# Gate one-hots split between VectorE and ScalarE, gate products as rounded part and rest, and PSUM sums copied out in the prompt attention

## What is computed

```python
# prompt attention, per head: softmax over causal keys, then the values
p = jax.nn.softmax(sc, axis=-1)            # sc = q.k/sqrt(dh) + bias
o = jnp.einsum("bhqk,bkhd->bqhd", p, v32)
# PEER, per token: 8 heads pick 16 experts each, out of 128 x 128
eidx = jnp.take_along_axis(cidx, pos, axis=-1)     # i1 * 128 + i2
g = jax.nn.softmax(top, axis=-1)
hid = jnp.einsum("thkd,td->thk", u_tab[eidx], xt)
a = g * jax.nn.gelu(hid, approximate=False)
out = jnp.einsum("thk,thkd->td", a, v_tab[eidx])
```

## Time and profile before

| | us |
|---|---|
| median of 3 runs (1883.18 to 1885.74) | 1885.15 |
| the profiled execution | 1886.61 |
| its span, first to last instruction | 1885.0 |

### The profile page before, as it was taken

The page is one execution under the profiler, slowest core; times in us unless marked ns, Lnnn a source line. Parts: engine busy times, 40 slices in busy tenths (PEclk is TensorE's granted clock), DMA queues, the critical chain, the costliest instruction groups (busy, mean ns, idle before and its releaser), DMA issues. The chain is left out here.

```text
span 1885.0 us, 30152 instructions
## 1 busy us (share of the span) xinstructions
PE 1701.0 (90%) x9914; PEld 1491.1 (79%) x9914; DVE 1438.2 (76%) x3371; ACT 683.1 (36%) x907; POOL 572.1 (30%) x508
## 2 busy tenths in 40 slices
PE   5997897779799999769989999998699999999995
PEld 3997643339699999769979999997588888888883
DVE  3334266524479989979989999997898999999985
ACT  3222032221434442344535455453333333333334
POOL 0010270000254543523333333333333333333330
PEclk8998898799799999979989999999799999999997
DMA  3242361152333332369997999999999999999992
GB/s 110 96 177 88 126 204 45 46 204 104 105 123 125 122 126 92 127 240 334 350 362 263 388 341 353 354 333 355 366 385 382 384 384 385 385 383 389 384 384 85
DMA packets 195214, 470.81 MB, mean 250 GB/s; under 512 B 17922, under 2 KB 100482, under 8 KB 192558
## 3 DMA queue, kind: packets, MB, share of 16 engines
q1 hardware_dynamic: 124014, 240.30, 36.1%
q0 software_dynamic: 50944, 178.96, 25.7%
q10 hardware_dynamic: 20160, 50.34, 6.9%
HBM read 411.97 MB, written 61.32 MB: 251 GB/s over the span
## 5 line engine op out<-in xcount | busy, mean ns | idle before, releaser
L226 PE MATMUL hp<-mid_hi,uhi 128*128 128x384 f32 x1024 | 355.8, 347 | 13.8 <-DVE ulo L1751 6.9
L227 PE MATMUL hp<-mid_lo,uhi 128*128 128x384 f32 x1024 | 346.6, 338 | 0.0
L228 PE MATMUL hp<-mid_hi,ulo 128*128 128x384 f32 x1024 | 345.1, 337 | 0.0
L226 PE MATMUL va<-vhi,ahi 128*128 128x512 f32 x768 | 299.7, 390 | 22.0 <-DVE alo L1957 22.0
L228 PE MATMUL va<-vhi,alo 128*128 128x512 f32 x768 | 299.5, 390 | 0.0
L227 PE MATMUL va<-vlo,ahi 128*128 128x512 f32 x768 | 299.5, 390 | 0.0
L1973 POOL DMA_INDIRECT gathered<-in_v_experts,idx_row x160 | 186.3, 1165 | 325.0 <-DVEq L1928 290.2
L1686 POOL DMA_INDIRECT gathered<-in_u_rows,idx_row x160 | 171.2, 1070 | 321.2 <-DVE hrow L1738 226.2
L226 PEld LDWEIGHTS hp<-mid_hi,uhi 128*128 128x128 f32 x1024 | 194.7, 190 | 18.0 <-DVE ulo L1751 9.1
L228 PEld LDWEIGHTS hp<-mid_hi,ulo 128*128 128x128 f32 x1024 | 194.3, 190 | 0.0
L227 PEld LDWEIGHTS hp<-mid_lo,uhi 128*128 128x128 f32 x1024 | 194.3, 190 | 0.0
(11 more groups left out here) (323 smaller groups left out, 3251.7 us busy)
## 6 DMA issues: line engine op xcount, KB each, us to landing
uw<-in_u_experts SPq DMA_DIRECT2D x128, 512.0 KB, 6.9
vw<-in_v_experts SPq DMA_DIRECT2D x128, 512.0 KB, 10.6
hidden_values<-gelu_out ACTq DMA_DIRECT2D x128, 192.0 KB, 5.9
gate_matrix<-gst ACTq DMA_DIRECT2D x12, 2048.0 KB, 13.2
mid_hi<-hidden_values SPq DMA_DIRECT2D x32, 768.0 KB, 11.9
mid_lo<-gate_matrix SPq DMA_DIRECT2D x32, 768.0 KB, 16.7
pw<-in_w_qk SPq DMA_DIRECT2D x16, 512.0 KB, 3.5
qw<-in_w_query SPq DMA_DIRECT2D x16, 512.0 KB, 4.7
```

Source lines behind the costliest of these rows:

```text
L226: nc.tensor.matmul(out, a_hi, b_hi, start=first, stop=False)
L227: nc.tensor.matmul(out, a_hi, b_lo, start=False, stop=False)
L228: return nc.tensor.matmul(out, a_lo, b_hi, start=False, stop=last)
```

## The change

In the gate stage:

- the transposed gates are kept as two parts: rounded to fp32r (by ScalarE) and the rest (by POOL). The transposed indices and gates lie over the used part of `I1`, `I2` and `GG`; `chunkT` has four columns a pick, copied by POOL in four pieces, with a new wait for ScalarE's progress (`first`)
- DVE builds `og` twice for each token, with the rounded gate and with the rest, and no `oh` any more; both in fp32r
- ScalarE builds `oh`: for each of four tokens |i - index| by an Abs with the index as bias (128 columns), then one Relu(1 - x) over the group's 512 columns, in fp32r. It does so two groups ahead, behind the copy of `gst`
- PE makes two fp32r products for each token, summed in PSUM, in place of one in fp32, and waits for `oh` and `first`.

In the prompt attention:

- ScalarE copies `DN` and `OT` out of PSUM (`move(j - 1)`, ahead of pair j's exponentials), and PE's `values(j, 0)` waits for that (`moved`) in place of `normed`
- DVE takes the reciprocal in two halves (`invert`), after blocks 0 and 1, and multiplies after block 1, both from SBUF; `split_hi` and `split_lo` come one block later
- the diagonals of pairs 4 to 7 are made by ScalarE, block by block
- `on` has two buffers; the copy of `OT` and the squares lie in a used part of `qkT`.

```diff
-            on = sb(st, "on", [P, SEQ])
-            sqt = sb(st, "sqt", [P, SEQ])
+            on = sb(st, "on", [P, 2, SEQ])
+            sqt, o_raw = qkT[:, 0, :SEQ], qkT[:, 1, :SEQ]
...
                     if i == 0 and j:
-                        pe.wait_ge(normed, j)
+                        pe.wait_ge(moved, j)
...
+                def invert(j, part):
+                    cols = slice(part * SEQ // 2, (part + 1) * SEQ // 2)
+                    dve.wait_ge(moved, j + 1)
+                    nc.vector.reciprocal(on[:, j % 2, cols], on[:, j % 2, cols]).then_inc(inv, 1)
+
                 def keep(j):
-                    dve.wait_ge(pv_mm, QB * (j + 1))
-                    if j:
-                        dve.wait_ge(o_lo, j)
-                    nc.vector.reciprocal(on[:], DN[:]).then_inc(inv, 1)
-                    dve.wait_ge(inv, j + 1)
-                    nc.vector.tensor_tensor(on[:], OT[:], on[:], ALU.mult).then_inc(normed, 1)
+                    dve.wait_ge(inv, 2 * (j + 1))
+                    nc.vector.tensor_tensor(on[:, j % 2], o_raw, on[:, j % 2], ALU.mult).then_inc(normed, 1)
...
-                        if i == 0 and j:
+                        if i < 2 and j:
+                            invert(j - 1, i)
+                        if i == 1 and j:
                             keep(j - 1)
-                        if i == 2 and j:
+                        if i == 3 and j:
                             split_lo(j - 1)
...
+                def diagonal(j, i):
+                    for u in range(2):
+                        act.wait_ge(max_done, unit(j, i, u) + 1)
+                        act.wait_ge(t_mm, unit(j - 2, QB - 1, u) + 1)
+                        last = nc.scalar.activation(diag[:, j % 2, u, i], ident[:], ACT.Copy, scale=negm[:, j % 2, u, i:i + 1])
+                        if i == QB - 1:
+                            last.then_inc(diag_done, 1)
...
+                def move(j):
+                    act.wait_ge(pv_mm, QB * (j + 1))
+                    if j:
+                        act.wait_ge(normed, j)
+                    if j >= 2:
+                        act.wait_ge(o_lo, j - 1)
+                    nc.scalar.activation(on[:, j % 2], DN[:], ACT.Copy)
+                    nc.scalar.activation(o_raw, OT[:], ACT.Copy).then_inc(moved, 1)
...
-            oh = sb(st, "oh", [P, RING, 4, P])
-            og = sb(st, "og", [P, RING, 4, P])
+            oh = sb(st, "oh", [P, RING, 4, P], F32R)
+            og = sb(st, "og", [P, RING, 4, 2, P], F32R)
...
                         pe.wait_ge(s["oh"], j * N2 + i + 1)
+                        pe.wait_ge(s["first"], j * N2 + i + 1 + GR)
                         pe.wait_ge(s["ev"], j * N2 + i + 1)
                         for k in range(4):
-                            last = nc.tensor.matmul(gp[i % 2][:, k], oh[:, i % RING, k], og[:, i % RING, k], start=True, stop=True)
+                            for q in range(2):
+                                last = nc.tensor.matmul(gp[i % 2][:, k], oh[:, i % RING, k], og[:, i % RING, k, q],
+                                                        start=q == 0, stop=q == 1)
...
-                    nc.gpsimd.tensor_copy(chunkT[:, u], slotT[:, :, bass.ds((2 * j + u) * CH, CH)]).then_inc(s["cut"], 1)
+                    if not first:
+                        pool.wait_ge(s["first"], (2 * j + u) * GR)
+                    for q in range(4):
+                        last = nc.gpsimd.tensor_copy(chunkT[:, u, q], GATES[q][:, bass.ds((2 * j + u) * CH, CH)])
+                    last.then_inc(s["cut"], 1)
...
-                        nc.vector.tensor_scalar(oh[:, i % RING, k], iota[:], col(1), None, ALU.is_equal)
-                        last = nc.vector.tensor_scalar(og[:, i % RING, k], iota[:], col(0), col(2), ALU.is_equal, ALU.mult)
+                        for q in range(2):
+                            last = nc.vector.tensor_scalar(og[:, i % RING, k, q], iota[:], col(0), col(2 + q), ALU.is_equal, ALU.mult)
...
+                def first_one_hot(j, i):
+
+                    u, r = groups[i]
+                    act.wait_ge(s["cut"], 2 * j + u + 1)
+                    act.wait_ge(s["mm"], j * N2 + i + 1)
+                    for k in range(4):
+                        last = nc.scalar.activation(oh[:, i % RING, k], iota[:], ACT.Abs, scale=-1.0,
+                                                    bias=chunkT[:, u, 1, 4 * r + k:4 * r + k + 1])
+                    last.then_inc(s["dist"], 1)
+                    act.wait_ge(s["dist"], j * N2 + i + 1)
+                    nc.scalar.activation(oh[:, i % RING], oh[:, i % RING].bitcast(F32), ACT.Relu, scale=-1.0, bias=1.0).then_inc(s["first"], 1)
...
                         nc.scalar.activation(gst[:, u, :, 4 * r:4 * r + 4].rearrange("p i t -> p t i"), gp[i % 2][:],
                                              ACT.Copy).then_inc(s["ev"], 1)
+                        if i + 2 < N2:
+                            first_one_hot(j, i + 2)
+                        elif not last:
+                            first_one_hot(j + 1, i + 2 - N2)
```

More of the change, by code:

```diff
@@ L675, in build @@
             stg = [sem(f"a_stg{u}") for u in range(4)]
-            s_mm, max_done, diag_done, t_mm, biased, e_done, pv_mm, inv, normed, o_hi, o_lo, summed, const_ld, const_ev = (
-                sem("a_" + n) for n in ("s_mm", "max", "diag", "t_mm", "biased", "e", "pv", "inv", "normed", "o_hi", "o_lo", "summed",
+            s_mm, max_done, diag_done, t_mm, biased, e_done, pv_mm, inv, moved, normed, o_hi, o_lo, summed, const_ld, const_ev = (
+                sem("a_" + n) for n in ("s_mm", "max", "diag", "t_mm", "biased", "e", "pv", "inv", "moved", "normed", "o_hi", "o_lo", "summed",
                                         "const_ld", "const_ev"))
@@ L865, in split_lo @@
                             dve.wait_ge(summed, j // 4 * 3 + j % 4 - 1)
[L866 removed]
+                        nc.vector.tensor_tensor(sqsum[:, j // 4], sqsum[:, j // 4], sqt, ALU.add).then_inc(summed, 1)
                 for i in range(QB):
@@ L895, in split_hi @@
                         act.wait_ge(summed, j // 4 * 3 + j % 4 - 1)
-                    nc.scalar.activation(sqt[:] if j % 4 else sqsum[:, j // 4], on[:], ACT.Square)
-                    nc.scalar.activation(mid_hi[:, j, :SEQ], on[:], ACT.Copy, scale=gO[:, j:j + 1]).then_inc(o_hi, 1)
+                    nc.scalar.activation(sqt if j % 4 else sqsum[:, j // 4], on[:, j % 2], ACT.Square)
+                    nc.scalar.activation(mid_hi[:, j, :SEQ], on[:, j % 2], ACT.Copy, scale=gO[:, j:j + 1]).then_inc(o_hi, 1)
+                def move(j):
[6 more added lines that the diff above has]
+                    nc.scalar.activation(o_raw, OT[:], ACT.Copy).then_inc(moved, 1)
                 for j in range(PAIRS):
+                    if j:
+                        move(j - 1)
                     for i in range(QB):
@@ L912, in _ @@
                                 nc.scalar.activation(ET[:, u, at[i]:at[i + 1]], ST[u][:, :n], ACT.Exp, scale=1.0 / SCALE8).then_inc(e_done, 1)
-                        if i == 1 and j:
+                        if j + 1 >= FOX and j + 1 < PAIRS:
+                            diagonal(j + 1, i)
+                        if i == 2 and j:
                             split_hi(j - 1)
+                move(PAIRS - 1)
                 split_hi(PAIRS - 1)
@@ L1612, in build @@
             tp = gp[0][:].rearrange("p a n -> p (a n)")[:, :TD]
-            names = ("tr", "trev", "cut", "oh", "mm", "ev", "part", "x2p", "tab", "idx", "dot", "hrow", "act")
+            names = ("tr", "trev", "cut", "oh", "dist", "first", "ghi", "glo", "mm", "ev", "part", "x2p", "tab", "idx", "dot", "hrow", "act")
             s = {n: sem("g_" + n) for n in names}
@@ L1787, in _ @@
                     act.wait_ge(s["tr"], i + 1)
-                    nc.scalar.activation(slotT[:, i], tp, ACT.Copy).then_inc(s["trev"], 1)
+                    if i == 2:
+                        nc.scalar.activation(rounded, tp.rearrange("p (a n) -> p a n", a=3), ACT.Copy).then_inc(s["ghi"], 1)
+                    nc.scalar.activation(slotT[i], tp, ACT.Copy).then_inc(s["trev"], 1)
                 act.wait_ge(x2r_spread, 16 * SG)
@@ L1793, in _ @@
                 act.sem_inc(stored[1], 16)
+                act.sem_inc(s["first"], GR)
+                def first_one_hot(j, i):
[8 more added lines that the diff above has]
+                    nc.scalar.activation(oh[:, i % RING], oh[:, i % RING].bitcast(F32), ACT.Relu, scale=-1.0, bias=1.0).then_inc(s["first"], 1)
+                first_one_hot(0, 0)
+                first_one_hot(0, 1)
                 def turn(j, half, last):
```

23 lines of the change are left out of this document (18 added, 5 removed).

## The result

| | before | after |
|---|---|---|
| median us | 1883.18 (1878.19 to 1885.74, 5 runs) | 1900.62 (1898.56 to 1906.16, 5 runs) |
| the profiled execution | 1886.61 | 1906.16 |
| its span | 1885.0 | 1904.5 |

The ratio is 1.0101, with a 95% interval of 1.0085 to 1.0117: 19.0 us slower (16 to 22). The spans differ by 19.5. The forecast was +19.9. Both profiled executions are the longest of their kernel's five runs, 3.4 us over the median before and 5.5 after.

What follows compares the result with a forecast made beforehand. It took DVE and PE to share the gate stage's bound, with DVE's lateness showing on PE. One-hots +23.4, waits -1, start +2 and attention -4.5 summed to +19.9 on 1885.15, giving 1905 us, range 1890 to 1926.

Steps and rivals of the forecast that it cites:

- Gate products on PE: Gate stage: 768 fp32r products replace 384 fp32 ones at the same 0.11 us load pace, 0; bounds -43 and +1.
- One-hots on VectorE: Gate stage: eight `og` replace four `oh` and four `og` a group, +0.244 us each over 96 groups, +23.4 us.
- First one-hots on ScalarE: Gate stage: four Abs and a Relu cost ScalarE 1.8 us a group, bounds 1.3 and 2.2; 29 us a turn.
- fourth rival: Gate stage: Abs or Relu outside Gelu's table forces two 1.28 us loads a group, some 2110 us in all; chance 0.02.
- The cover of 2.7 us: Gate stage: 2.7 us spare between tiles covers ScalarE's lateness of up to 1.8 us while DVE sets the pace.
- The prediction's own signs of being wrong: Gate stage: wrong if ScalarE has no idle time left in a turn, or DVE's falls under 1 us a turn.
- Waits in the stage: Gate stage: slower DVE steps shorten waits for gathers and `uhi`, late ScalarE work takes it back; -1, bounds -28 and +22.
- first rival: Gate stage: ScalarE becomes the bound, a turn of 83 in place of 76.9, giving 1920 us; chance 0.18.
- a turn of 80 to 81: Gate stage sign: a turn takes 80 to 81 us, with DVE over 96% busy and PE waiting for `og`.
- Start of the stage: Gate stage start: extra POOL passes, copies and two ScalarE groups stand ahead of the first work; +2, bounds 0 and +4.
- Prompt attention: Prompt attention: waits of `OT` -5.1, clock -1.8 and +1.0, tail +1.4, sum -4.5; bounds -9 and +1.4.
- Moving the diagonals: Prompt attention: moving the diagonals to ScalarE frees DVE only where it waits anyway, 0.

Runs made afterwards that it cites:

- one product: The changed kernel with PE multiplying only with the rounded gate's one-hot, the product with the rest left out: ratio 1.0055.
- all `oh` in fp32: Kernel before plus attention half, with ScalarE building all `oh`, each `og` built once and one fp32 product kept: ratio 0.9978, 1879.1 us.
- one `og`: The changed kernel with VectorE building only the rounded gate's one-hot, used by both products, the rest of the gates left out: ratio 1.0024.
- no Relu: The changed kernel without ScalarE's Relu, so `oh` keeps the distances: ratio 1.0037.
- the gate half: The kernel before with only the gate-stage half of the change: ratio 1.0135, +25.4 us.
- half of `oh` on ScalarE: Kernel before plus attention half, one fp32 product kept, ScalarE building two of each four `oh` and VectorE the others: ratio 0.9901, 1864.6 us.
- both engines relieved: The changed kernel with one `og` a token and without the Relu, both parts of the computation left out: ratio 0.9902.

## Why the prediction was right, step by step

**The time was right and the sum's largest term too; the cover behind it was not there, and the attention was mis-sized.** Term by term:

*Gate products on PE, 0: right.* Eight loads still take 0.97 us, 0.111 apart, and with four of them 0.52, (0.52 - 0.19)/3 = 0.11. The loads of after, then of the kernel with one product:

```profile
1195.83 0.97 PEld L1696 LDWEIGHTS ggp<-og,oh 128*128 128x128 f32 x8 [0.90 <-DVE og L1774]
```

```profile
1185.44 0.52 PEld L1695 LDWEIGHTS ggp<-og,oh 128*128 128x128 f32 x4 [1.36 <-DVE og L1773]
```

By the Trainium skill's four passes for true fp32 (FP8 and Floating Point Precision, TensorE Precision Notes) the prediction put PE's gain at up to 43 us; the run with all `oh` in fp32 against the one with one `og` in fp32r shows no loss, and the loads start at the same pace in both forms. The Trainium skill's load time by columns, 107 ns for 128 (TensorE: Matmul & The Clock Gate, LDWEIGHTS), agrees with the 0.11 us of the traces, for fp32 and fp32r alike.

*One-hots on VectorE, +23.4: right.* Sixteen `og` of after start 4.11 us before what follows them, 0.257 each, 2.05 a group:

```profile
1193.54 4.19 DVE L1774 TENSOR_SCALAR og<-iota,chunkT 128x128 fp32r<-128x128 f32 x16
1197.65 1.21 DVE L1783 CUSTOM_DVE_ANT_0 gathered<-gathered,x2p 128x1024 f32<-128x1024 f32 x1
```

*First one-hots on ScalarE, 1.8 us a group: right,* to 1.80: four Abs 1.26 (1192.43 to 1193.69), the Relu 0.54 (1161.11 to 1161.65 in the kernel with one `og`, where the next gelu follows at once). No table load falls in the gate stage, and the fourth rival is out; that agrees with the Trainium skill (ScalarE: Activation LUTs, Table sets: the hidden batching unit), which has abs and relu in every set. One tile and its group of after:

```profile
1190.57 1.06 ACT L1316 ACTIVATE uhi<-uw 128x1024 fp32r<-128x1024 f32 x1 [0.47 <-ACT gelu_out L1336]
1191.54 1.12 ACT L1876 ACTIVATE gst<-ggp 128x512 f32<-128x512 f32 x1
1192.43 1.23 ACT L1849 ACTIVATE oh<-iota,chunkT 128x128 fp32r<-128x128 f32 x4
1193.69 0.63 ACT L1853 ACTIVATE oh<-oh 128x512 fp32r<-128x512 f32 x1
1195.29 0.49 ACT L1336 ACTIVATE gelu_out<-hp 128x384 f32<-128x384 f32 x1 [0.96 <-PE hp L228]
```

The step said that no row shows an Abs. That was a slip: the trace of before has one (L568, 8 x 544, 0.66 us, with no table load between it and the function ahead). Its shape is far from this one, so the bounds would have stayed. The fourth rival's "eight Squares" are six in the earlier trace rows; nothing hangs on that.

*The cover of 2.7 us: this step failed.* The prediction added up ScalarE's path to 74 us a turn, 78 with the waits for stores, and VectorE's to 78.5, and took the larger. The numbers were good: alone, VectorE's chain makes a turn of 78.7 (no Relu) and ScalarE's one of 80.3 (one `og`). With the cover, VectorE would have set the pace and taking the Relu off ScalarE would have given next to nothing. It gave 12 us: in the fifth turn VectorE waits 4.2 us for `uhi` in the whole change and not at all without the Relu. And taking half of the `og` off VectorE, with ScalarE's work left whole, gave 14.5: 2.0 and 2.4 a turn. Each engine holds the other up, and neither alone sets the pace. By the times the turn is thus some 2 us longer than either chain alone; the traced turns say 3 with the whole change and nothing with the gate half (80.3), so the size of it is not settled by them. Why the cover fell short was not measured. It was reckoned from one tile's mean times, as if VectorE and PE were always on time, and the tiles of a turn differ (one or two groups, one or two dots); that is the likely reason. The point from which ScalarE decides was put at 2.1 us a group; at 1.80 it held the turn up about as much as VectorE did.

The prediction's own signs of being wrong didn't show this: in the fifth turn ScalarE still waited 6.9 us for PE, and VectorE was idle for 4.9.

*Waits in the stage, -1: right in size by luck of two parts.* VectorE's waits went from 30.4 us to 30.9: those for gathers fell by 8.7, and those for `uhi` grew by 9.4. The six turns grew by 1.2, 6.5, 0.5, 5.8, 6.4 and 2.7 us where the prediction had 3.9 for each. In that trace turns 2, 4 and 5 look like the first rival (a turn of 83), and VectorE is busy 94% of the fifth, not over 96%. But the trace of the gate half alone has 81.3, 81.0 and 80.3 for the same turns, with VectorE busy 98% of the fifth, which is the forecast's picture. So "a turn of 80 to 81" came true in one of the two traces and not in the other, and these two can't tell the forecast from its first rival by the turn. The time can: the rival's 1920 is far off.

*Start of the stage, +2: right* (2.1).

*Prompt attention, -4.5: mis-sized, -8.7 in the trace and -9.6 by the ratio.* The wait of `OT` for VectorE went, all 5.1 us of it, as it should. The clock was the term that was mis-sized. The rows for the first `OT` of pairs 4 to 7 of after (of before, have pairs 4 and 6; all four take 1.97 or 1.98):

```profile
294.02 1.08 PE L800 MATMUL OT<-ET,v 128*64 128x512 f32 x4
...
311.67 1.98 PE L800 MATMUL OT<-ET,v 128*64 128x512 f32 x4
...
328.94 1.98 PE L800 MATMUL OT<-ET,v 128*64 128x512 f32 x4
...
344.05 1.08 PE L800 MATMUL OT<-ET,v 128*64 128x512 f32 x4
```

Between these four starts, before and then after (columns: us, PE busy, granted clock, DMA share, GB/s):

```profile
294.55:314.73 20.18, 15.13 (x72) 0.84 0.17 53
314.73:334.31 19.58, 14.49 (x73) 0.85 0.12 41
334.31:352.43 18.12, 14.87 (x64) 0.78 0.00 1
```

```profile
294.02:311.67 17.65, 13.51 (x73) 0.88 0.20 61
311.67:328.94 17.27, 14.05 (x74) 0.90 0.13 46
328.94:344.05 15.11, 12.61 (x65) 0.93 0.00 1
```

Of the 7.9 us that these three lost, PE's idle time gave 3.5 (13.4 to 9.9; the three waits of `OT` were 3.2) and its busy time 4.3, for the same work at a higher mean clock. In the last blocks, from the last of these starts to the end of the last `DN`, it is another 1.5 (8.4 to 6.9 us, at a granted clock of 0.80 and then 1.00). That makes 5.8 from the clock, where the prediction had 1.8 - 1.0. It had reckoned that the clock stays down in pairs 5 to 7; in pair 7 `OT` takes 1.08, in nine of the eleven kernels with the copies, and 1.97 or 1.98 in the three without. The 1.98 in pair 4 before, from which it took its 1.8, was the chance of one execution: with only the diagonals moved, and the wait of `OT` still there, it is 1.08. The tail beyond `DN` was priced at +1.4 and is +1.1. With -5.1 and -5.8 the three make -9.8; the traces have -10.3 from the first `OT` on. The attention began 1.0 us earlier, and 2.6 were lost in pair 0 (13.8 to 16.4 us from the first scores to the first `OT`), where PE's work is the same, the granted clock was 0.75 and then 0.57, and the kernels here took 13.6 to 18.0 us: in all -8.7. "Moving the diagonals: 0" failed too, as shown above.

**Why the total came out right.** The attention gained 4.2 more than forecast; the gate stage (+23.0 against 22.4) and the stages that nothing touches (+3.0) took 3.6 back. The attention's error was hidden in part by what one execution differs from another: the ratios of the halves are -9.6 and +25.4 where the forecast had -4.5 and +24.4, and they add to +15.8 beside the forecast's 19.9.

## What to carry to other kernels

Where work passes round a ring of engines, add up each engine's whole chain of a turn, its own gaps and DMA waits in it, before giving it more: here, with chains of 77 to 80 us, none hid behind the others, and relieving either of two gave 2 us a turn. Moving work to an idle engine has a best dose: here half of `oh` on ScalarE gave 9 us, and all of it cost 5. Where a change moves work and also changes its form, run the move alone: with the fp32 product kept it was 23 us faster than with the gates split in two. And two steps that relieve one engine may be worth more together than each alone adds up to, so price them together.

## What the runs showed of the hardware

- VectorE stops once for long behind the second turn, where the kernel's hardware loop goes round (idle ahead of `ulo` 6.86 us before, 7.22 after, 11.4 in the kernel with both engines relieved), and turn 3 is the longest in every kernel (83.4 to 93.7). After names no wait for it ("issue"), and before puts PE's 6.2 us there down to "issue" too; its cause wasn't looked into.
- A one-hot with two pointer operands takes VectorE 0.257 us whether it writes fp32 or fp32r, and one with a single pointer 0.20.
- A 128x128 product in fp32 and two in fp32r take PE the same, 0.22 us (eight loads in 0.97 us for four tokens in either form, 0.11 apart).
- In the prompt attention, 5.1 us less waiting went with 5.8 us less of PE's busy time for the same work, in one trace of each; the granted clock of the three stretches rose from 0.84, 0.85 and 0.78 to 0.88, 0.90 and 0.93.
